# One unused matrix product ahead of the attention scores of ten pairs of heads in a hybrid decoder layer

## The reference

```python
y_ssm  = _s5_mixer(u, ...)                       # scan over 512 steps, then a gated linear layer
qr, kr = _rope(_rmsnorm(q, ...)), _rope(_rmsnorm(k, ...))
s_idx  = einsum('bths,bth->bts', relu(einsum('bthd,bsd->bths', qir, kir)), wi)
_, sel = lax.top_k(s_idx, 128)                   # per query, causal
p      = softmax(einsum('bthd,btkhd->bhtk', qb, kg) * scale)   # over the chosen keys
y_attn = einsum('bhtk,btkhd->bthd', p, vg)
h = x + g1 * (concat(_rmsnorm(y_ssm), _rmsnorm(y_attn)) @ w_out)
h = h + g2 * (gelu(gate) * val) @ w_down         # after w_up and a causal convolution
```

## Time and profile before

| | us |
|---|---|
| median of 3 runs | 793.03 |
| lowest and highest | 785.03, 793.17 |
| the profiled execution, its own time | 793.33 |
| its span, from the first to the last instruction | 791.5 |

### The profile page before, as it was taken

The page is one execution under the profiler, slowest core; times in us unless marked ns, Lnnn a source line. Parts: engine busy times, 40 slices in busy tenths (PEclk is TensorE's granted clock), DMA queues, the critical chain, the costliest instruction groups (busy, mean ns, idle before and its releaser), DMA issues.

```text
span 791.5 us, 9897 instructions
## 1 busy us (share of the span) xinstructions
PE 724.9 (92%) x3564; PEld 580.2 (73%) x3564; DVE 466.0 (59%) x831; ACT 337.9 (43%) x508; POOL 266.0 (34%) x209
## 2 busy tenths in 40 slices
PE   0899999998687889889979999999999999999998
PEld 0786877777574566768769788888887887888886
DVE  4859687976999496958661576755445554000005
ACT  3534346745422453533255654454455544211110
POOL 1004798329702100000021434433443344334440
PEclk9989999999777859789989999999999999999999
DMA  8942231260273453661820332233323322233112
GB/s 301 377 119 64 72 106 54 81 187 0 30 76 51 154 212 107 265 266 54 313 85 1 107 106 75 84 106 106 105 64 97 106 83 76 107 107 106 65 43 106
DMA packets 63016, 91.46 MB, mean 116 GB/s; under 512 B 11946, under 2 KB 41410, under 8 KB 62915
## 3 DMA queue, kind: packets, MB, share of 16 engines
q1 hardware_dynamic: 59456, 89.44, 35.7%
q10 hardware_dynamic: 3523, 1.54, 0.7%
HBM read 86.28 MB, written 4.69 MB: 115 GB/s over the span
## 4 chain that ended last, share of the span: by engine, by line
PE 80%; DVE 12%; ACT 4%; issue 2%; DMA 1%; ACTq 0%; SPq 0%; DVEq 0%
PE bank L1576 23%; PE bank L1578 22%; PE bank L1577 22%; PE bank L1581 3%; PE bank L1919 2%; DVE arena L1285 1%; DVE stat L1282 1%; PE bank L1807 1%; PE bank L1607 1%; DMA xh<-in_x 1%; PE bank L1914 1%; PE bank L1586 1%; PE bank L1787 1%; DVE stat L1069 1%; DVE arena L1150 1%
## 5 line engine op out<-in xcount | busy, mean ns | idle before, releaser
L481 POOL TENSOR_TENSOR w_lo<-w_raw,w_hi 128x2048 fp32r<-128x2048 f32 x34 | 156.8, 4612 | 401.7 <-ACT w_hi L675 200.0
L1576 PE MATMUL bank<-act_hi,w_hi 128*128 128x512 f32 (+2 forms) x384 | 148.9, 388 | 6.3 <-DVE act_lo L1513 4.7
L1577 PE MATMUL bank<-act_lo,w_hi 128*128 128x512 f32 (+2 forms) x384 | 147.7, 385 | 0.0
L1578 PE MATMUL bank<-act_hi,w_lo 128*128 128x512 f32 (+2 forms) x384 | 147.4, 384 | 0.0
L1576 PE MATMUL bank<-w_hi,act_hi 128*128 128x512 f32 x240 | 102.8, 428 | 1.6 <-DVE act_lo L1179 1.6
L1577 PE MATMUL bank<-w_lo,act_hi 128*128 128x512 f32 x240 | 98.2, 409 | 0.0
L1578 PE MATMUL bank<-w_hi,act_lo 128*128 128x512 f32 x240 | 98.1, 409 | 0.0
L1576 PEld LDWEIGHTS bank<-act_hi,w_hi 128*128 128x128 f32 x384 | 73.6, 192 | 21.6 <-issue 5.4
L675 ACT ACTIVATE w_hi<-w_raw 128x2048 fp32r<-128x2048 f32 x26 | 49.7, 1913 | 88.4 <-PE bank L1578 87.0
L1577 PEld LDWEIGHTS bank<-act_lo,w_hi 128*128 128x128 f32 x384 | 73.6, 192 | 14.7 <-issue 0.2
L1578 PEld LDWEIGHTS bank<-act_hi,w_lo 128*128 128x128 f32 x384 | 73.6, 192 | 14.5
(11 more groups left out here) (301 smaller groups left out, 1194.4 us busy)
## 6 DMA issues: line engine op xcount, KB each, us to landing
w_raw<-in_w_up SPq DMA_DIRECT2D x44, 512.0 KB, 4.6
arena<-in_w_ada SPq DMA_DIRECT2D x6, 2048.0 KB, 15.6
w_raw<-in_w_down SPq DMA_DIRECT2D x22, 512.0 KB, 4.0
w_raw<-in_w_in SPq DMA_DIRECT2D x10, 1024.0 KB, 5.1
arena<-in_w_ada SPq DMA_DIRECT2D x8, 1024.0 KB, 6.6
xh<-in_x SPq DMA_DIRECT2D x8, 512.0 KB, 8.3
w_raw<-in_w_out SPq DMA_DIRECT2D x4, 1024.0 KB, 12.1
s_mem<-in_w_ada SPq DMA_DIRECT2D x4, 1024.0 KB, 7.3
```

The source lines that it names most:

```text
L481: nc.gpsimd.tensor_tensor(w_lo[:, slot, 0:width], w_raw[:, slot, 0:width], w_hi[:, slot, 0:width].bitcast(F32), ALU.subtract).then_inc(S[" ...
L1576: T.matmul(dst, lhs_hi, rhs_hi, start=start, stop=False)
L1577: T.matmul(dst, lhs_hi, rhs_lo, start=False, stop=False)
L1578: return T.matmul(dst, lhs_lo, rhs_hi, start=False, stop=stop)
```

## The change

A tuple `KEEP_BUSY` names ten even units: 8, 10, 12, 14, 16, 18, 20, 22, 28 and 30. Ahead of the scores of each of these pairs TensorE gets one more float32 product: the turned keys of the first two heads (`k_t[:, 0, :]`, 128 x 512) with the identity as the stationary operand. It goes to bank 2, all 512 columns. Nobody reads the result, and the next `turn_probs` of an even unit writes the bank anew. The product has no wait of its own and signals nothing. It stands ahead of the wait of `logits`, so it starts as soon as TensorE is done with the values before it.

```diff
+KEEP_BUSY = (*range(8, 24, 2), 28, 30)
 OUT_BANK = ((4, 6, 7, 5), (0, 1, 2, 3))
...
+            def keep_busy(i):
+
+                T.matmul(bank[2 + i % 2][:], ident[:], k_t[:, 0, :], start=True, stop=True)
+
             for i in range(0, ATT_UNITS + 4, 2):
                 if i < ATT_UNITS:
+                    if i in KEEP_BUSY:
+                        keep_busy(i)
                     logits(i)
                     logits(i + 1)
```

## The result

| | before | after |
|---|---|---|
| median of 20 runs each, us | 786.25 | 782.25 |
| lowest and highest, us | 782.63, 793.29 | 777.11, 792.06 |
| ratio, 95% interval | | 0.9938, 0.991 to 0.9966 |
| profiled execution: its own time, us | 793.33 | 778.69 |
| its span, us, and mean granted clock | 791.5, 0.944 | 776.9, 0.974 |

The account below looks back on a forecast made before the run. TensorE was taken to bound most of the kernel, alternating with VectorE and ScalarE in the attention stage. 793.33 + 0.2 + 1.76 - 1.5 - 1.5 - 2.2 = 790.1 us, less 0.3 gives 789.8; range 783 to 796.

Parts of the forecast that it names:

- The base: Starting time of the sum: the profiled execution's 793.33 us, with the median of the runs shown 0.3 us lower.
- What bounds, and the price: Attention stage alternates between late VectorE, TensorE and ScalarE; one product costs 0.88 to 1.05 us at upper clock, 1.76 at lower.
- Unit 8: Product ahead of scores that VectorE reads at 202.79 us: cost 0 to 0.3 us, taken as 0.2.
- Units 10 to 16: Products ahead of the first `y`, all fitting into TensorE's waits: cost 0.
- First half of `y`: Clock expected still down at 243.3 us: gain 0 taken, 2.8 us the bound.
- Unit 18 and the second `y`: Product on the path, costing 1.76 us; clock rising sooner in the second half of `y`, giving back 1.5 us.
- First glu: Fall of the clock not prevented, but the stretch from 277 us mixed: half of 3.0 us taken, 1.5 us gained.
- End of the loop: Products of units 28 and 30 fill the wait ahead, so the faster clock gains all 2.2 us.
- Behind the loop: Outside the attention stage, where nothing is edited: no term; a time change there would show the prediction wrong.
- The clock stays up through the whole stage: Rival: all four slow stretches gain 10.9 us, unit 18's product is paid, giving 783.1 us; chance 0.17.
- The clock doesn't care: Rival: the clock's falls stay and unit 18's product is paid, giving 794.3 to 795.0 us; chance 0.20.
- The slow rival: Rival: products run at the lower clock on the path, also at units 20, 22, 28 and 30: 798.5 us; chance 0.08.

Follow-up runs that it names:

- e5_change: The unaltered change measured again against the kernel before, on another chip beside other variants; ratio 0.9910 (0.9873 to 0.9946).
- e4_1216: Kernel before plus only the products of units 12, 14 and 16; ratio 1.0015 (0.9976 to 1.0054).
- e1_early: Kernel before plus only the products of units 8, 10, 12, 14 and 16; ratio 0.9895 (0.9831 to 0.9959).
- e2_only8: Kernel before plus only the product of unit 8; ratio 0.9989 (0.9950 to 1.0028).
- e4_18: Kernel before plus only the product of unit 18; ratio 0.9973 (0.9934 to 1.0013).
- e1_late: Kernel before plus only the products of units 18, 20, 22, 28 and 30; ratio 0.9987 (0.9947 to 1.0026).
- e3_glu3: Kernel before plus only three products, in the wait ahead of the first glu; ratio 0.9930 (0.9887 to 0.9972).
- e3_2830: Kernel before plus only the products of units 28 and 30; ratio 0.9991 (0.9954 to 1.0028).
- e1_tiny: The change with its ten products cut from 512 to 8 columns; against the kernel before, ratio 0.9996 (0.9958 to 1.0034).
- e3_more: Kernel before plus products filling TensorE's waits, unit 8's product, and eight unused 128-column products after the loop; ratio 0.9852 (0.9811 to 0.9894).
- e1_fill: Kernel before plus products where TensorE waits, also ahead of turned probabilities and the first glu, none at units 8 and 18; ratio 0.9909 (0.9874 to 0.9944).

## Why the prediction was wrong, step by step

- **The base.** The step that failed in absolute terms is "793.33 (the profiled execution's own time)" and the median 0.3 us beside it. The kernel's own median is 786.25, so 6.8 of the 7.5 us are there. The prediction did say that the three runs spread over 8 us, but it widened the range by 1 us for that and not by 7, and only around sums that started at the slow end. The difference itself was forecast at 3.2 us and measured at 4.9 (7.1 in e5_change), but it is made up otherwise than forecast, as follows.
- **What bounds, and the price.** Right: the stage alternates as told, and a product costs 1.01 us at the upper level (forecast 0.88 to 1.05) and up to 1.96 where the clock is down (1.76).
- **Unit 8.** "Taken as 0.2", measured 0.92 us of waiting by VectorE. The cover was thinner than in the trace read: there VectorE's step ahead of the mask step took 1.62 us, here 0.61. The loss may have come back as the missed collision with GpSimd, which the working didn't have.
- **Units 10 to 16.** Cost 0, right.
- **First half of `y`.** "0 taken, 2.8 the bound": this is the mis-sized term. The first `y` ran at 1.00 in both profiles of the change, and y1 to y2 took 13.1 us and not 16.1: -3.1 us, where the sum has +1.76 for the product of unit 18 and nothing against it. For the products of 12 to 16 alone the 0 was right (e4_1216, 16.1 us). How much of the 3.1 us the products made and how much the place of the falls is open (e1_early, e2_only8).
- **Unit 18 and the second `y`.** "+1.76 - 1.5": the gain has the right size, 1.7 us from y2 to glu in the change and in e4_18. In e4_18 it came as the working says, with the clock down from 256 us on and back at 260, when the second `y` starts; in the change there was no fall to come back from, and in e1_late the product brought nothing there (32.1 us). The price was taken at the lower level; it was 1.01 us in the change and 1.1 in e4_18.
- **First glu.** "-1.5": nothing, 19.8 us after and 19.6 before. The prediction's own remark was right, that no product stands in the wait ahead of it; the half taken in spite of it was not. With products there it is 2.9 us (e3_glu3).
- **End of the loop.** "I take all 2.2 us": 0.7 us in the profiles (25.3 and 26.0), and 26.0 in e3_2830, which has those two products alone. The fall came anyway.
- **Behind the loop.** Nothing in the sum, 5.3 us less in the profile after than in that before. Two of the prediction's own signs of being wrong came true: this one, and VectorE's wait for scores before 243 us (unit 8).
- **The rivals.** "The clock stays up through the whole stage" is the nearest: it held for both `y` and not for the `glu` and the loop's end. Its 783.1 us is close to the result by luck, by two errors that cancel: a gain of 9.9 us instead of about 5, from a base 6.8 us too high. "The clock doesn't care" is refuted by e1_tiny against the change, and by e3_glu3. The slow rival didn't occur.

What stays open is the part behind the loop. It takes 448.7 to 449.9 us in ten profiles and 451.7 to 455.3 in the other ten, although nothing is edited there. All of the former have a product ahead of the scores of 18 or of the turned probabilities of 15, and none of the latter but e3_more. The clock falls in different places there, once in the short ones and two to four times in the long; why was not tried. Of the 14.6 us between the two profiled spans 4.0 lie ahead of the first `y`, 5.3 between it and the end of the loop and 5.3 behind the loop, so how the measured 4.9 us divide is not known.

## What to carry to other kernels

Before a sum is built on a profiled execution, place that execution in the scatter of its kernel: here one kernel spread over 12 us, more than twice what the edit brought. One profile per kernel shows where the clock fell in that execution and not where it falls in all. Unused work can raise TensorE's clock where it stands in a wait ahead of the work that counts, even if it only brings the clock back in time. Behind the wait, where TensorE is late, it costs its price and can bring about as much back (1.1 and 1.7 us for unit 18). Keep a copy with next to no work in it as the control, and try the set and its parts with enough executions to tell them apart.

## What the runs showed of the hardware that was not expected

- TensorE's clock was at 0.50 while three unused products ran, and at 1.00 when the `glu` began behind them (e3_glu3, 16.6 us from glu to glu4 and not 19.6). That is as good as in e1_fill, where the clock was at 1.00 from 282.2 us on and it took 16.7.
- A VectorE addition on 32 partitions and 64 elements took 0.2 us when it fell at the gap between two GpSimd instructions of 2.0 to 2.4 us, and up to 2.1 us when it fell onto one; it then ended within 0.1 us of the GpSimd instruction's end. The pair that started at 206.05 us in e1_tiny was done at 209.23, the pair that started at 206.87 in the change at 207.22.
